# Late columns gated on GpSimd, 35 tiles in the first pass, two pairs in the third slot, gathers paced 1.15 pairs a tile, the first norm's fillers during the loads

## The reference

```
x = x + mixers(rms_norm(x) @ w_in) @ w_out        # HGRN2, dilated attention, Mamba2
x = x + peer_ffn(rms_norm(x), w_query, sub_keys, down, up)
peer_ffn: q = x @ w_query; s = q . sub_keys        # 8 heads, 2 x 128 keys
          top 16 of the 2 lists, top 16 of their 256 sums -> idx, gate
          a = down[idx] . x ; c = gate * gelu(a) ; out = sum c * up[idx]   # 16384 experts
```

## Time and profile before

| | |
|---|---|
| median of 3 runs | 2409.53 us (2408.37 to 2410.78) |
| the profiled execution: time, span | 2411.78 us, 2410.0 us |
| busy share PE, DVE, ACT, POOL | 96%, 57%, 22%, 10% |
| first passes (L881) | 221.7 to 527.3 us, 1057.5 to 1363.1 us |
| second passes (L903) | 527.3 to 839.4 us, 1363.1 to 1674.4 us |
| transfers of 1024 KB in the two expert layers | 256 pair loads, 208 gathers |

### The profile page before, as it was taken

The page is one execution under the profiler, slowest core; times in us unless marked ns, Lnnn a source line. Parts: engine busy times, 40 slices in busy tenths (PEclk is TensorE's granted clock), DMA queues, the critical chain, the costliest instruction groups (busy, mean ns, idle before and its releaser), DMA issues.

```text
span 2410.0 us, 35607 instructions
## 1 busy us (share of the span) xinstructions
PE 2319.3 (96%) x14194; PEld 1946.6 (81%) x14194; DVE 1378.5 (57%) x3065; ACT 542.2 (22%) x1763; POOL 245.2 (10%) x272
## 2 busy tenths in 40 slices
PE   8999999998989999999999989999999999999998
PEld 7558999998888875599999988888866667776665
DVE  5745898984444467368889744444453332464333
ACT  2122225530111121322355301101210001351001
POOL 0000122111111000011221111110000000000000
PEclk9999999999999999999999999999999999999999
DMA  6213999999999923049999999999335342304441
GB/s 233 105 70 149 362 386 406 400 404 421 421 421 420 385 107 134 35 180 379 391 406 393 411 421 420 421 420 367 140 140 209 152 162 75 136 1 179 171 173 54
DMA packets 88306, 642.27 MB, mean 267 GB/s; under 512 B 11931, under 2 KB 14530, under 8 KB 15694
## 3 DMA queue, kind: packets, MB, share of 16 engines
q1 hardware_dynamic: 55660, 420.85, 44.0%
q0 software_dynamic: 31488, 218.34, 22.2%
q10 hardware_dynamic: 994, 0.82, 0.1%
HBM read 638.69 MB, written 1.06 MB: 265 GB/s over the span
## 4 chain that ended last, share of the span: by engine, by line
PE 79%; DMA 16%; DVE 3%; ACT 1%; issue 0%; POOL 0%; POOLq 0%; SPq 0%; DVEq 0%; PEldq 0%
PE bank L881 22%; DMA weight_ring<-in_experts 16%; PE bank L572 10%; PE bank L592 9%; PE bank L903 9%; PE bank L609 8%; PE bank L537 4%; PE bank L892 3%; PE bank L799 2%; PE bank L494 2%; PE bank L1084 1%; PE bank L561 1%; PE bank L1128 1%; PE bank L645 1%; DVE arena L1766 1%; PE bank L498 1%
## 5 line engine op out<-in xcount | busy, mean ns | idle before, releaser
L903 PE MATMUL bank<-arena,weight_ring 128*128 128x152 f32 x4096 | 556.6, 295 | 52.8 <-DMA weight_ring<-in_experts 52.6
L903 PEld LDWEIGHTS bank<-arena,weight_ring 128*128 128x128 f32 x4096 | 534.8, 190 | 77.9 <-DMA weight_ring<-in_experts 42.2
L881 PE MATMUL bank<-hidden_T,weight_ring 128*128 128x152 f32 x4096 | 544.5, 293 | 0.0
L881 PEld LDWEIGHTS bank<-hidden_T,weight_ring 128*128 128x128 f32 x4096 | 533.1, 190 | 0.9
L1909 DVE CUSTOM_DVE_ANT_0 arena<-arena 128x1024 f32<-128x1024 f32 x208 | 254.4, 1223 | 317.9 <-DMA arena<-in_expert_rows,choice_by_pair 317.3
L1211 POOL DMA_INDIRECT arena<-in_expert_rows,choice_by_pair x208 | 202.0, 971 | 913.4 <-DVE arena L1922 776.8
L1922 DVE SCALAR_TENSOR_TENSOR arena<-arena,pair_weights 128x1024 f32<-128x1024 f32 x202 | 258.9, 1282 | 15.7 <-ACT pair_weights L1384 15.2
L572 PE MATMUL bank<-hidden_T,weight_ring 128*128 128x256 f32 (+1 forms) x1024 | 233.2, 387 | 5.6 <-DVE hidden_T L1610 5.3
L572 PEld LDWEIGHTS bank<-hidden_T,weight_ring 128*128 128x128 f32 (+1 forms) x1024 | 192.3, 190 | 40.0 <-DVE hidden_T L1610 6.7
L1382 ACT ACTIVATE pair_weights<-pair_dots 128x1 f32<-128x1 f32 x208 | 42.0, 202 | 528.8 <-DVE pair_dots L1909 528.8
L609 PE MATMUL bank<-arena 128*128 128x512 f32 x352 | 160.8, 592 | 0.0
(11 more groups left out here) (366 smaller groups left out, 2329.9 us busy)
## 6 DMA issues: line engine op xcount, KB each, us to landing
weight_ring<-in_experts SPq DMA_DIRECT2D x256, 1024.0 KB, 11.3
weight_ring<-in_dense_h SPq DMA_DIRECT2D x22, 2048.0 KB, 7.9
weight_ring<-in_mlp SPq DMA_DIRECT2D x32, 1024.0 KB, 6.9
arena<-in_mlp SPq DMA_DIRECT2D x32, 1024.0 KB, 6.8
weight_ring<-in_dense_nsa SPq DMA_DIRECT2D x9, 2048.0 KB, 7.8
weight_ring<-in_dense_rg SPq DMA_DIRECT2D x7, 2048.0 KB, 8.3
arena<-in_expert_rows,choice_by_pair POOLq DMA_INDIRECT x208, 12.1
arena<-distance_bias_scratch SPq DMA_DIRECT2D x2, 768.0 KB, 7.0
```

Source lines behind the costliest of these rows:

```text
L881: last = mm(bank[s % 3][:, 0:DT_TOK], w[:, k * P:(k + 1) * P], HT[:, k, 0:DT_TOK], start=k == 0, stop=k == KD - 1)
L903: last = mm(bank[4 + k // 2][:, (k % 2) * DT_TOK:(k % 2 + 1) * DT_TOK], w[:, k * P:(k + 1) * P], HACT[:, s, :], start=s == 0 and k % 2 == ...
```

## The change

1. `late(s)` moves from DVE to POOL, between the gathers: POOL's program now goes through steps 64 to 127, late(s) first, then a gather if s is in `LATE_TILES`. 16 gathers stand ahead of it, 53 behind it.
2. `LATE_TILES` has 35 entries instead of 32, one every 1.83 steps. 48 dots now stand ahead of the second pass.
3. The gathers of the second pass are paced 1.15 pairs a tile instead of 1.1, and the last waits for pair 60 instead of 58. PE waits for all tiles after step 126 instead of 125.
4. The first two pairs of layer 0 (pairs 2 and 3 of layer 1) go to the two halves of slot 2, so that six pair loads stand ahead of the first that waits for a step; from there on the ring has four buffers as before. The slot order of section 1 is turned so that the slots come free in this order.
5. `X` comes in two halves with a semaphore each, ACT starts a half's squares when that half is there, blocks 1 and 2 are issued only when block 0 has landed, and PE runs 16 fillers on a zeroed `pick_eight` before the identity is there, and none behind it.

```diff
--- before.py
+++ after.py
@@ -55,14 +55,14 @@
 CUT = tuple(HALF + 3 + 31 * n // 20 for n in range(GROUPS))
-LATE_TILES = range(HALF, NKEYS, 2)
+LATE_TILES = [HALF + 64 * n // 35 for n in range(35)]
 ROUTE_ORDER = (1, 0)
...
 MOVE_AT = 2 * 4
-LAST_GATHER_AT = 58
+LAST_GATHER_AT = 60
 WIDE, NARROW = 4, 4
@@ -71,7 +71,7 @@
 SECTION_BLOCKS = (HYBRID_BLOCKS, HYBRID_BLOCKS, RG_BLOCKS_N, NSA_BLOCKS)
-SLOT_ORDER = ((0, 1, 2), (2, 0, 1), (2, 1, 0), (0, 1, 2))
+SLOT_ORDER = ((0, 1, 2), (2, 1, 0), (2, 1, 0), (0, 1, 2))
 
@@ -90,7 +90,18 @@
 def buffer_of(layer, i):
-    return (i + 2 * layer) % RING
+    spare = i - 2 * layer
+    if 0 <= spare < 2:
+        return RING + spare
+    return i if i < 2 else (i + 2) % RING
+
+
+def earlier_in_buffer(layer, i):
+    return [n for n in range(i) if buffer_of(layer, n) == buffer_of(layer, i)]
+
+
+def pair_loads(layer, i):
+    return 16 * (len(earlier_in_buffer(layer, i)) + 1)
 
@@ -115,7 +126,7 @@
 
-    return LAST_GATHER_AT - (TILES - 1 - j) * 11 // 10
+    return LAST_GATHER_AT - (TILES - 1 - j) * 115 // 100
 
@@ -342,6 +353,7 @@
         first_loaded = ctx.enter_context(nc.semaphore("first_loaded"))
+        rows_loaded = [ctx.enter_context(nc.semaphore(f"rows_loaded{tt}")) for tt in range(TT)]
         const_loaded = ctx.enter_context(nc.semaphore("const_loaded"))
@@ -414,14 +426,14 @@
                 for i in range(PAIRS):
-                    r = buffer_of(l, i)
-                    if i < RING:
+                    r, earlier = buffer_of(l, i), earlier_in_buffer(l, i)
+                    if not earlier:
 
                         sp.wait_ge(S["proj_done"], 2 * last_in_slot[r // 2] + 2)
-                    elif i < PAIRS // 2 + RING:
-                        sp.wait_ge(S["hidden_ready"], 2 * (i - RING + 1))
+                    elif earlier[-1] < PAIRS // 2:
+                        sp.wait_ge(S["hidden_ready"], 2 * (earlier[-1] + 1))
                     else:
-                        sp.wait_ge(S["step_used"], i - RING + 1 - PAIRS // 2)
+                        sp.wait_ge(S["step_used"], earlier[-1] + 1 - PAIRS // 2)
                     sp.dma_start(ring[:, r * 2048:(r + 1) * 2048], load(i)).then_inc(S[f"step_loaded{r}"], 16)
@@ -442,7 +454,9 @@
             hybrid_block = [lambda b: I["dense_h"][0, b], lambda b: I["dense_h"][1, b]]
-            sp.dma_start(X[:], I["x"].rearrange("b (t p) d -> p (b t) d", p=P)).then_inc(first_loaded, 16)
+            x = I["x"].rearrange("b (t p) d -> p (b t) d", p=P)
+            sp.dma_start(X[:, 0, :], x[:, 0, :]).then_inc(rows_loaded[0], 16)
+            sp.dma_start(X[:, 1, :], x[:, 1, :]).then_inc(rows_loaded[1], 16)
             sp.dma_start(ident[:], I["c_ident"]).then_inc(first_loaded, 16)
@@ -450,6 +464,7 @@
             sp.dma_start(arena[0:NUM_BUCKETS + 1, 31700:31700 + 384], I["c_bucket"]).then_inc(const_loaded, 16)
+            sp.wait_ge(block_loaded[0], 16)
             block(0, 1, hybrid_block[0])
@@ -494,7 +509,7 @@
             def norm(count, spare=1):
-                for _ in range(12):
+                for _ in range(0 if spare is None else 12):
                     mm(bank[spare][:, 0:P], ident[:], ident[:], start=True, stop=True)
@@ -619,11 +634,14 @@
 
-            pe.wait_ge(first_loaded, 32)
+            pe.wait_ge(one_ready, 2)
+            for _ in range(16):
+                mm(bank[5][:, 0:P], pick8[:], pick8[:], start=True, stop=True)
+            pe.wait_ge(first_loaded, 16)
 
...
                 subk = subks[:, l, :]
-                norm(0, 5)
+                norm(0, 5 if l else None)
 
@@ -870,7 +888,7 @@
                     i, r = s // 2, buffer_of(l, s // 2)
-                    pe.wait_ge(S[f"step_loaded{r}"], 16 * (i // RING + 1))
+                    pe.wait_ge(S[f"step_loaded{r}"], pair_loads(l, i))
 
@@ -943,7 +961,7 @@
                             mm(bank[2 + q][GT0 - P:P, :], fold[:, 0:64], ACC[:, 0, q * 512:(q + 1) * 512], start=True, stop=True)
-                    if s == NKEYS - 3:
+                    if s == NKEYS - 2:
 
@@ -1188,9 +1206,8 @@
 
-                move(0)
-                pool.wait_ge(pack_moved, 16 * (24 * l + 2))
-                for j in range(TILES):
+                def gather(j):
+
                     if j == MOVE_AT:
@@ -1211,6 +1228,26 @@
                                                 pair_loaded[j % GBUF], 16)
+
+                def late(s):
+
+                    g = gated_before(s)
+                    pool.wait_ge(S["hidden_kept"], put_by(s))
+                    nc.gpsimd.tensor_tensor(HACT[:, s, 0:g], LATE[:, s % 3, 0:g], HACT[:, s, 0:g], ALU.mult).then_inc(S["late_gated"], 1)
+
+                move(0)
+                pool.wait_ge(pack_moved, 16 * (24 * l + 2))
+                j = GBUF + sum(ROUTE_TILES) + 3
+                for n in range(j):
+                    gather(n)
+                for s in range(HALF, NKEYS):
+                    if s > CUT[0]:
+                        late(s)
+                    if s in LATE_TILES:
+                        gather(j)
+                        j += 1
+                for j in range(j, TILES):
+                    gather(j)
             for section in range(DEPTH, DEPTH + 2):
@@ -1229,7 +1266,9 @@
                     for c in range(2):
-                        if added:
+                        if added is None:
+                            act.wait_ge(rows_loaded[tt], 16)
+                        else:
                             act.wait_ge(added, 2 * tt + c + 1)
@@ -1258,7 +1297,6 @@
             root_ahead()
-            act.wait_ge(first_loaded, 32)
 
@@ -1629,7 +1667,7 @@
             V.memset(stat[:, 253:254], 1.0).then_inc(one_ready, 1)
-            dve.wait_ge(first_loaded, 32)
+            V.memset(pick8[:], 0.0).then_inc(one_ready, 1)
 
@@ -2073,20 +2111,12 @@
 
-                def late(s):
-
-                    g = gated_before(s)
-                    dve.wait_ge(S["hidden_kept"], put_by(s))
-                    V.tensor_tensor(HACT[:, s, 0:g], LATE[:, s % 3, 0:g], HACT[:, s, 0:g], ALU.mult).then_inc(S["late_gated"], 1)
-
                 onehots(0)
...
                 for s in range(HALF, NKEYS):
-                    if s > CUT[0]:
-                        late(s)
                     for n in range(GROUPS):
```

2 lines of the change are left out of this document (1 added, 1 removed).

## The result

The changed kernel takes 2402.11 us in the median (five runs, 2399.60 to 2407.48), against 2408.37 us for the kernel before, run beside it (2407.50 to 2410.78). The ratio is 0.9976, 95% interval 0.9965 to 0.9988: a gain of 6 us, where 19 were forecast. The time lies inside the range; the size of the gain is a third of the one I worked out. The profiled execution took 2399.6 us, the fastest of the five; its span is 2397.8 us. So the two profiles stand 12.2 us apart and not 6.3, and their stages say where: 7.9 us in the two second passes, 4.4 us behind the second of them and 1.7 us between the two layers; ahead of the first expert pass the changed kernel takes 1.8 us more.

What follows compares the result with a forecast made beforehand. PE was taken to bound the first pass, transfers the second. Two layers at -11.6 + 1.5 + 1.5 us and -2.0 for the start gave -19.2 us: 2390 us in the median, range 2381 to 2406.

Steps and rivals of the forecast that it cites:

- The bound, and a gather's worth: Second pass bound by transfers, first by PE; a gather taken out of the second pass is worth 2.49 us.
- What the first pass must carry: Three more transfers in the first pass just fit; charged +1.5 us of backlog a layer, between 0 and 7.5.
- the lag of VectorE: VectorE falls behind with its tiles in the first pass: +1.5 us a layer, between 0 and 5.4.
- my own formula: Time per tile in the gather loop: 2.8 us plus landing, over 3; 4.0 to 5.0 us against 4.69 available.
- The last gather later: End of second pass: 117.5 transfers instead of 119, ending at 827.8 instead of 839.4 us, -11.6 us with the gathers.
- PE waits at most 1 us ahead of L968: Sign that the forecast is right: PE waits no longer than 1 us there.
- L921's idle for weights: Sign in the second pass: PE's idle for weights falls from 27.4 to about 16 us a layer.
- The start: Program start, once: earlier X and no fillers behind the identity give -2.0 us, between -4 and 0.
- Late on GpSimd: First pass: one late multiplication takes 0.4 us on GpSimd; VectorE falls from 136.5 to 130.8 us busy.
- two pairs in slot 2: First pass: pairs come earlier, but PE waits for no weights there: 0.
- the first rival: VectorE and GpSimd block each other, 15%: late multiplications stop VectorE for 22 us at 0.4 us each; 2394 to about 2405.
- No effect: Rival, 7%: 401 GB/s is already the first pass's limit, the three transfers return as wait; 2403 to 2409 us.

Runs made afterwards that it cites:

- e9: The kernel before with one line changed, 35 late tiles instead of 32, late multiplications still on VectorE: 2395.3 us, ratio 0.9943.
- e7: The changed kernel with the next section's block 0 held until the last gather has landed, and 32 late tiles instead of 35: 2409.5 us.
- e8: The changed kernel with block 0 held until the last gather has landed, 38 late tiles instead of 35 and 1.2 pairs a tile: 2398.2 us.
- e13: e9 with the changed end alone (last gather at pair 60, 1.15 pairs a tile, fold after step 126): 2400.6 us.
- e2: The changed kernel with the old end (last gather at pair 58, 1.1 pairs a tile, fold after step 125): 2399.3 us.
- e3_late_dve: The changed kernel with the late multiplications back on VectorE, 35 tiles kept: 2404.3 us.
- e1_old_start: The changed kernel with the old start (X in one load, blocks 1 and 2 issued at once, twelve fillers behind the identity): 2402.4 us.
- e10: The changed kernel with block 0 held, 12 fillers ahead of the first projection, and late multiplications back on VectorE: 2390.4 us.
- e6: The changed kernel with block 0 held until the last gather has landed and the old pair buffers, no spare pairs in slot 2: 2399.4 us.
- e16: e9 with the new start and fillers, block 0 held, last gather at pair 60, 1.15 pairs a tile, fold behind step 127: 2387.8 us.

## Why the prediction was wrong, step by step

**The bound, and a gather's worth: right.** Three gathers a layer taken out of the second pass were put at 7.5 us. The 35 tiles alone shortened the second passes by 7.0 and 6.2 us (e9), going back to 32 lengthened them by 7.2 and 6.4 (e7): 2.1 to 2.4 us a gather.

**What the first pass must carry, and the lag of VectorE: wrong, on the safe side.** I charged 1.5 + 1.5 us a layer. Neither shows: 305.4 us in each of the sixteen kernels with 32 or 35 tiles. Landings rose from 9.3 to 10.6 us in the median, as I had expected in kind, and by my own formula that is (2.8 + 10.6) / 3 = 4.5 us a tile, below the 4.69 at hand. The edge is real and lies between 35 and 38: 38 tiles want one every 4.3 us (4.69 x 35/38), the landing there was 11.2 us (e8), and the formula gives 4.7. It fits; that this loop and nothing else sets the edge, no run shows.

**The last gather later: this is the step that failed.** "Three fewer, but with the last gather two pairs later 1.5 more" and an end at 827.8 us were a count of bytes alone. The count left out that the gather is tied to PE's own step: it is issued when pair 60 is used, and the fold stands behind step 126. In the changed kernel PE gets from the issue to the fold in 826.7 - 812.98 = 13.7 us. My own rows had the gather's need: 12.2 us of landing and 3.8 to be weighed, 16.0 us. So PE had to wait for at least 2.3 us; before, with 833.15 - 811.78 = 21.4 us, there was room. Counted from the start of the second pass of layer 0, the gather is issued at 278.2 us in e9 and at 284.8 in e13, at 279.1 in e2 and at 284.1 in the changed kernel: the two pairs of PE moved it by 5.0 to 6.6 us, where 1.5 transfers are 3.7, and it landed at 297.7 us, where my count had 292.6. Block 0's 2048 KB in front of the gather added 1.4 us of landing. And the clock fell behind the wait, for 1.7 us more. Forecast for this part: about -4 us a layer (11.6 less 7.5). Measured: +2.7 and +2.3 (e13). I had written "PE waits at most 1 us ahead of L968" as a test of it; 3.8 and 2.4 us answered. The other signs said the same: L921's idle for weights is 20.0 and 20.7 us a layer, not about 16, and the second passes, counted to the end of the last step, took 307.4 and 308.4 us, not 300 to 304.

**The start: wrong in size and sign.** I took -2.0 us from one profile. Three more kernels with the old start have their projection at 14.42, 14.79 and 13.46 us instead of 15.85: the one I read was the slowest of four. The bias product began at 28.6 us in the mean of those four, at 29.8 in the mean of the nine with the new start, at 28.2 in the five with the new start and fillers. In eight of the nine the 64 records of the projection took 15.4 to 16.9 us; in the ninth (e3_late_dve), and in all nine with fillers or the old start, 14.1. The Trainium skill (TensorE: Matmul & The Clock Gate, Part 4: PE-mode transpose) says that transposes do not count as activity; its result for this start, nothing gained, is what was measured, and these eight agree; the ninth, with the same transposes and 3.21 us of idle, does not. That it was the transposes and not the idle 3 us behind them, no run here separates. And the earlier trace rows misled me: their 1.00 is no reading. The first record of the clock in the trace of before is a rise to 1.00 at 13.4 us, just when the slow fillers ended; in e1_old_start it stands at 10.9 us, and there the fillers, from 7.37 us on, took 4.64 us instead of 5.49.

**Late on GpSimd, two pairs in slot 2.** The size of one late was near enough (0.51 us in the median, 0.4 taken). That VectorE would fall to 130.8 us was wrong; the same stretch as in the earlier trace rows is now

```profile
373.00:521.80 148.80, 140.94 (x197) 1.00 1.01 416
```

10.1 us above it: contention gave the time back. It did no harm and no good, and it was not needed for the 35 tiles (e9, e10). The spare pairs were put at 0; e6 and e16 allow 0 to 3 us for them, and that stays open.

**The sum again, from profiles:** -13.2 for the gathers (e9), nothing for the charges, +5.0 for the end (e13), +1.1 for the start (the two means above): -7.1 us. The median says -6.3; with single profiles behind each term, that they agree so well is partly luck. The forecast was -15.0, +6.0, -8.2 and -2.0. So the end alone is 13.2 us off, more than the whole miss of 12.9, and the charges that nothing answered to hid 6 us of it: that the time still lies inside the range is owed to them in part, and is luck.

**The rivals.** None of them was it. The contention was there, at 10.1 us of VectorE where the first rival had 22, and it never reached PE. No effect in the first pass is refuted by 415 GB/s. The wait that took the place of the one removed, at the fold, was not among them.

## What to carry to other kernels

Where a transfer's issue is tied to a consumer's step, write the two times beside each other before counting bytes: from that step to the place where its result is needed, and landing plus work on it. Put the instruction that waits for the last transfer behind everything that doesn't need it, and let no large transfer that can wait go ahead of it. In a change of several parts, run the one-line part alone: here it was worth twice the whole.

## What was not expected of the hardware

A wait of PE can cost more than itself. Of the seven waits ahead of the fold that were 3.8 us or longer, the granted clock fell to 0.50 in or behind all seven; of the fifteen between 1.2 and 2.7 us, behind five (2.1 to 2.7 us long); of the fourteen ends of a second pass with a wait of 0.3 us or none, in none. Each fall was about 3.4 us long or more and cost 1.7 us or more. It also falls with PE busy without a gap: at 108 to 112 us, for 3.4 to 6.9 us, in 13 of the 18 profiles, at a place that the change does not touch (12.28 us of one group of 28 records became 13.98).

Such falls are a good part of why the runs of one kernel are 2 to 13 us apart. In every kernel the runs with the lower mean granted clock tend to be the longer ones: of the changed kernel's five, 2407.48 us stands at 0.991, 2402.96 at 0.993, the other three (2399.60 to 2402.11) at 0.994, and 0.003 of 2400 us is 7.2. They fit the places at which the two profiles differ outside the second passes, too: between the layers the profile before has two falls and the changed one has one; behind the second pass of layer 1 it is three against one, the last few us of the program left out; ahead of the first pass the changed one has the fall at 110.9 us that the other lacks.
